# Diagonal score blocks of the recurrent pairs made in the projection phase, with the first four half pairs inverted there on GpSimd

## The reference, cut to what matters

```python
def step(s, inp):
    r_t, w_t, k_t, v_t, a_t, b_t = inp
    sa = jnp.einsum('bhvk,bhk->bhv', s, a_t)
    s = s * w_t[:, :, None, :] + sa[..., None] * b_t[:, :, None, :] + v_t[..., None] * k_t[:, :, None, :]
    return s, jnp.einsum('bhvk,bhk->bhv', s, r_t)
```

## Time and profile before

| | |
|---|---|
| median of 3 runs | 3104.68 us (3103.49 to 3105.19) |
| span of the profiled execution | 3097.4 us |
| median less that span | 7.3 us |
| PE busy | 2577.9 us, 83% |
| DVE busy | 1596.9 us, 52% |
| GpSimd busy | 740.9 us, 24% |
| granted clock of PE, mean | 0.902 |

### The profile page before, as it was taken

One profiled execution on the slowest core, in us unless ns is written; L12 is line 12 of the kernel. 1 busy time (PEld: TensorE's weight loads), 2 busy tenths in 40 slices (PEclk: granted clock), 3 DMA queues, 4 the chain that ended last, 5 costly groups with the idle time before them and its releaser, 6 DMA issues. The chain is left out here.

```text
span 3097.4 us, 54814 instructions
## 1 busy us (share of the span) xinstructions
PE 2577.9 (83%) x23550; PEld 2183.5 (70%) x23550; DVE 1596.9 (52%) x2411; ACT 902.7 (29%) x1464; POOL 740.9 (24%) x739
## 2 busy tenths in 40 slices
PE   6899999974788854676775999999599999998787
PEld 2577677764677753456564777877499999998665
DVE  3037887542435624785465556465544546454233
ACT  2114333311132222563202232222233333332211
POOL 1111111116556641111322111111021111111421
PEclk8999999986889887677887999999799999999898
DMA  6622555532324313121461323232402222210521
GB/s 263 223 65 80 165 146 158 165 129 77 80 73 127 103 30 97 37 54 32 155 133 55 112 97 116 97 109 99 176 35 76 89 76 90 76 55 2 220 94 60
DMA packets 291551, 319.51 MB, mean 103 GB/s; under 512 B 109807, under 2 KB 235190, under 8 KB 288750
## 3 DMA queue, kind: packets, MB, share of 16 engines
q1 hardware_dynamic: 290240, 312.64, 31.7%
q10 hardware_dynamic: 1070, 3.37, 0.3%
HBM read 203.32 MB, written 112.56 MB: 102 GB/s over the span
## 5 line engine op out<-in xcount | busy, mean ns | idle before, releaser
L2893 PE MATMUL PS<-Q,K 128*128 128x128 f32 x2560 | 296.3, 278 | 32.4 <-DMA K<-k_d 23.7
L2893 PEld LDWEIGHTS PS<-Q,K 128*128 128x128 f32 x2560 | 292.9, 194 | 34.9 <-issue 27.8
L3014 POOL TENSOR_TENSOR weights_lo<-weights,weights_hi 128x1664 fp32r<-128x1664 f32 x32 | 121.3, 3790 | 566.5 <-ACT weights_hi L2972 566.5
L2920 PE MATMUL PS<-V_hi,weights_hi 128*128 128x258 f32 x832 | 239.1, 287 | 5.4 <-DVE H L3123 2.7
L461 PE MATMUL PS<-hT_hi,w_in_hi 128*128 128x512 f32 (+1 forms) x640 | 239.7, 374 | 0.0
L462 PE MATMUL PS<-hT_lo,w_in_hi 128*128 128x512 f32 (+1 forms) x640 | 236.4, 369 | 0.0
L463 PE MATMUL PS<-hT_hi,w_in_lo 128*128 128x512 f32 (+1 forms) x640 | 236.2, 369 | 0.0
L2921 PE MATMUL PS<-V_lo,weights_hi 128*128 128x258 f32 x832 | 236.0, 284 | 0.0
L2922 PE MATMUL PS<-V_hi,weights_lo 128*128 128x258 f32 x832 | 235.3, 283 | 0.0
L461 PE MATMUL PS<-h_hi,w_in_hi 128*128 128x512 f32 (+1 forms) x624 | 228.5, 366 | 5.3 <-PEq L112 5.3
L2394 PE MATMUL PS<-w_out_hi,y_in_hi 128*128 128x512 f32 x416 | 169.0, 406 | 70.4 <-DVE y_in_lo L2332 39.1
(11 more groups left out here) (412 smaller groups left out, 5681.6 us busy)
## 6 DMA issues: line engine op xcount, KB each, us to landing
chunk_in<-in_d SPq DMA_DIRECT2D x40, 512.0 KB, 3.4
w_in<-in_e_w_in_dram SPq DMA_DIRECT2D x30, 512.0 KB, 5.0
xnew<-in_o_w_in_dram SPq DMA_DIRECT2D x30, 512.0 KB, 6.1
in_d<-xnat SPq DMA_DIRECT2D x20, 640.0 KB, 6.0
modw<-in_mod_w_dram SPq DMA_DIRECT2D x12, 1024.0 KB, 9.9
xnat<-in_mod_w_dram SPq DMA_DIRECT2D x8, 1536.0 KB, 7.2
v_d<-xnew SPq DMA_DIRECT2D x16, 640.0 KB, 3.0
k_d<-xc SPq DMA_DIRECT2D x16, 640.0 KB, 2.9
```

Source lines behind the costliest of these rows:

```text
L2893: last = pe.matmul(PS[:, 4 + x % 4, (j - j0) * P:(j - j0 + 1) * P], K[:, kt, j * P:(j + 1) * P], Q[:, kt, i * P:(i + 1) * P], start=(kt == ...
L2920: pe.matmul(out, wh, VH[:, j, q], start=(j == seen[0]), stop=False)
L3014: pool.tensor_tensor(WL[n % 2][:], W[:, n % 2], WH[n % 2][:].bitcast(F32), ALU.subtract).then_inc(s["w_lo"], 1)
```

## The change

The diagonal blocks are made a second time, in the projection phase: PE multiplies the 32-token blocks directly (`block_product`, `blk0` in tile b+4 and `blk1` in tile b+5), DVE masks them into `blocks_out` (`blocks`), and SP stores them (`blocks_away`). GpSimd inverts half pairs 0 to 3 there, ten of the 30 steps behind the low part of each tile from 13 to 24 (`invert`), with SP moving blocks in and results out (`inversion_io`). In the pair stage, `blocks_in` only loads (inverses for n below 4, blocks from 4 on), the transposed copy L1559 is gone, returning the blocks to `N` is a function of its own (`blocks_back`), and the inversion of half n+4 is started in turn n. The constants are cut into other pieces, so the masks of the pair stage are loaded at its start. The diff, cut:

```diff
-    PREP_PE[_b, 0], PREP_PE[_b, 1] = [("w0", _p)], [("a0", _p)]
+    PREP_PE[_b, 0], PREP_PE[_b, 1] = [("w0", _p)], [("a0", _p)] + ([("blk1", _p - 1)] if _p else [])
     PREP_PE[_b, 2] = [("bonus", _p - 1)] if _p else []
     PREP_PE[_b + 1, 0], PREP_PE[_b + 1, 1], PREP_PE[_b + 1, 2] = [("w1", _p)], [("a1", _p)], [("ksum", _p)]
+    PREP_PE[_b + 4, 1] = [("blk0", _p)]
+PREP_PE[PREP_AT + 4 * PREP_TILES, 1] = [("blk1", 3)]
...
-PREP_SEQ = [(name, p, i) for key in sorted(PREP_PE) for name, p in PREP_PE[key] for i in range(3)]
+PREP_SEQ = [(name, p, i) for key in sorted(PREP_PE) for name, p in PREP_PE[key] for i in range(2 if name[0:3] == "blk" else 3)]
...
+EARLY_HALVES = 4
+INVERT_AT, INVERT_TILES = 13, 3
+INVERT_STEPS = 30
...
+def invert_steps(pool, step, U, tmp, first, end, done=None, value=0):
+    for k in range(first, end, -1):
+        w = 31 - k
+        prod = tmp[0:104, 0:k * w].rearrange("b (i j) -> b i j", i=k)
+        step.link(pool.tensor_tensor(prod, U[0:104, 0:k, k:k + 1].broadcast_to([104, k, w]),
+                                     U[0:104, k:k + 1, k + 1:32].broadcast_to([104, k, w]), ALU.mult))
+        ins = pool.tensor_tensor(U[0:104, 0:k, k + 1:32], U[0:104, 0:k, k + 1:32], prod, ALU.add)
+        if k > 1:
+            step.link(ins)
+        else:
+            step.publish(ins, done, value)
...
+        U, blk = sb("early_blocks", [P, 32, 32]), sb("blocks_out", [P, NCH, 2, 32])
+        inv_tmp = G.c("pick")
...
+                def blocks_away(p, d):
+                    sp.wait_ge(s["by_dve"], BY_DVE.index((f"blk{d}", p, 1)) + 1)
+                    for i in range(2):
+                        for k in range(4):
+                            sp.dma_start(A.blk_d[2 * p + i, d, 10 * k:10 * k + 10].rearrange("b s t -> s b t"),
+                                         blk[32 * k:32 * k + 32, 5 * i:5 * i + 5].rearrange("s c h t -> s (c h) t")).then_inc(s["blk_st"], 16)
...
+                def inversion_io(n):
+                    i, at = divmod(n - INVERT_AT + 1, INVERT_TILES)
+                    if at or i < 0 or i > EARLY_HALVES:
+                        return
+                    if i:
+                        sp.wait_ge(s["inv_ok"], i)
+                        for d in range(2):
+                            sp.dma_start(A.inv_d[i - 1, d].rearrange("b s t -> b (s t)"),
+                                         U[64 * d:64 * d + 40].rearrange("b s t -> b (s t)")).then_inc(s["inv_st"], 16)
+                    if i < EARLY_HALVES:
+                        sp.wait_ge(s["blk_st"], 16 * 16 * (i // 2 + 1))
+                        if i:
+                            sp.wait_ge(s["inv_st"], 32 * i)
+                        else:
+                            sp.wait_ge(s["u_zero"], 1)
+                        for d in range(2):
+                            sp.dma_start(U[64 * d:64 * d + 40].rearrange("b s t -> b (s t)"),
+                                         A.blk_d[i, d].rearrange("b s t -> b (s t)")).then_inc(s["inv_in"], 16)
...
+                    if k < 2 and p:
+                        blocks_away(p - 1, k)
...
+                    inversion_io(n)
+                blocks_away(3, 1)
...
+                def block_product(p, d):
+                    ops = (aa[0], sg[0]) if d == 0 else (sg[1], kk)
+                    for h in range(2):
+                        x, bank = piece_of(f"blk{d}", p, h)
+                        bank_free(x)
+                        q = slice(64 * h, 64 * h + 64)
+                        for c in range(NCH):
+                            for k in range(4):
+                                t = slice(c * CH + 32 * k, c * CH + 32 * k + 32)
+                                ins = pe.matmul(PS[32 * k:32 * k + 32, bank, 32 * c:32 * c + 32], ops[0][q, t], ops[1][q, t],
+                                                start=True, stop=True)
+                        ins.then_inc(s["pp_ps"], 1)
...
+                            if name == "blk0":
+                                pe.wait_ge(ready[0], 4 * p + 3)
+                                block_product(p, 0)
+                            elif name == "blk1":
+                                pe.wait_ge(ready[1], 4 * p + 2)
+                                block_product(p, 1)
+                            else:
...
+                def invert(n):
+                    i, part = divmod(n - INVERT_AT, INVERT_TILES)
+                    if i < 0 or i >= EARLY_HALVES:
+                        return
+                    if part == 0:
+                        pool.wait_ge(s["inv_in"], 32 * (i + 1))
+                        inv_step.link(unit_diagonal(pool, U))
+                    each = INVERT_STEPS // INVERT_TILES
+                    invert_steps(pool, inv_step, U, inv_tmp, INVERT_STEPS - each * part, INVERT_STEPS - each * (part + 1), s["inv_ok"], i + 1)
...
+                pool.memset(U[:], 0.0).then_inc(s["u_zero"], 1)
                 for n in range(1, last + 1):
                     pool.wait_ge(s["hi_ok"], n)
                     pool.tensor_tensor(wl[n % 2][:], w[:, n % 2], wh[n % 2][:].bitcast(F32), ALU.subtract).then_inc(s["lo_ok"], 1)
+                    invert(n)
...
+                def blocks(p, d):
+                    if p or d:
+                        dve.wait_ge(s["blk_st"], 128 * (2 * p + d))
+                    for h in range(2):
+                        x, bank = piece_of(f"blk{d}", p, h)
+                        dve.wait_ge(s["pp_ps"], x + 1)
+                        dve.tensor_tensor(blk[:, :, h], PS[:, bank, 0:32 * NCH].rearrange("p (c t) -> p c t", t=32),
+                                          G.c("tri")[:, None, :].broadcast_to([P, NCH, 32]), ALU.mult).then_inc(s["by_dve"], 1)
...
+                        blocks(p - 1, 1)
...
+                        blocks(p, 0)
...
                 def blocks_in(n):
-                    sp.wait_ge(s["bx_sb"], HC * (n + 1))
+                    sp.wait_ge(s["zt_ok"], n)
+                    if n > EARLY_HALVES:
+                        sp.wait_ge(s["zu_st"], 32 * (n - EARLY_HALVES))
+                    src = A.inv_d if n < EARLY_HALVES else A.blk_d
                     for d in range(2):
-                        for k in range(4):
-                            sp.dma_start(A.blk_d[n, d, 10 * k:10 * k + 10].rearrange("b s t -> s b t"),
-                                         diag(d, n, k, k).rearrange("s c h t -> s (c h) t")).then_inc(s["rel_st"], 16)
-                    sp.wait_ge(s["rel_st"], 128 * (n + 1))
-                    if n:
-                        sp.wait_ge(s["zu_st"], 32 * n)
-                        sp.wait_ge(s["zt_st"], 32 * n)
-                    for d, dst in enumerate((U, Ut)):
-                        sp.dma_start(dst[64 * d:64 * d + 40].rearrange("b s t -> b (s t)"),
-                                     A.blk_d[n, d].rearrange("b s t -> b (s t)")).then_inc(s["rel_in"], 16)
+                        sp.dma_start(U[64 * d:64 * d + 40].rearrange("b s t -> b (s t)"),
+                                     src[n, d].rearrange("b s t -> b (s t)")).then_inc(s["rel_in"], 16)
...
-                    sp.wait_ge(s["inv_ok"], n + 1)
-                    away(U, A.inv_d, s["zu_st"])
+                    if n >= EARLY_HALVES:
+                        sp.wait_ge(s["inv_ok"], n - EARLY_HALVES + 1)
+                        away(U, A.inv_d, s["zu_st"])
                     sp.wait_ge(s["zt_ok"], n + 1)
                     away(Ut, A.invt_d, s["zt_st"])
...
+                    sp.wait_ge(s["bx_sb"], HC * (n + 1))
                     if n:
                         sp.wait_ge(s["y64_ps"], n)
-                    sp.wait_ge(s["zu_st"], 32 * (n + 1))
+                    else:
+                        sp.wait_ge(s["zero"], 4)
+                    if n >= EARLY_HALVES:
+                        sp.wait_ge(s["zu_st"], 32 * (n - EARLY_HALVES + 1))
...
+                sp.dma_start(G.cst_rwkv[:], A.consts[:, G.ends[3]:G.ends[4]]).then_inc(s["consts"], 16)
                 for m in half_chunks(0):
                     load(m)
+                sp.wait_ge(s["zero"], 1)
+                for d in range(2):
+                    sp.dma_start(U[64 * d:64 * d + 40].rearrange("b s t -> b (s t)"),
+                                 A.inv_d[0, d].rearrange("b s t -> b (s t)")).then_inc(s["rel_in"], 16)
...
-                sp.wait_ge(s["zero"], 4)
+                for n in range(EARLY_HALVES):
+                    blocks_out(n)
+                    blocks_in(n + 1)
+                blocks_back(0)
                 sp.wait_ge(s["wa_zero"], 1)
-                blocks_in(0)
-                blocks_out(0)
...
-                    if n + 1 < HALVES:
-                        blocks_in(n + 1)
...
-                        blocks_out(n + 1)
+                        blocks_back(n + 1)
+                    if n + EARLY_HALVES < HALVES:
+                        blocks_out(n + EARLY_HALVES)
+                        if n + EARLY_HALVES + 1 < HALVES:
```

(41 more changed lines are left out.)

52 lines of the change are left out of this document (31 added, 21 removed).

## The result

The changed kernel takes 3130.86 us (median of 4 runs, 3128.47 to 3132.05) against 3104.93 us before in the same measurement: the ratio is 1.0083 with a 95% interval of 1.0070 to 1.0096, so it is 26 us slower. The forecast was 13 us faster, and 3130.86 lies above the range's end of 3125, 39 us above the forecast of 3092.

The account below looks back on a forecast made before the run. PE bounds the projection nearly end to end, while the pair stage has 172 us of idle PE, 89.7 of it waiting for inverted blocks. 3097.4 - 113 (gain) + 100 (loss) + 7.3 gave 3092 us, range 3055 to 3125.

Parts of the forecast that it names:

- the 7.3 us around the span: Whole kernel: the median lies 7.3 us above the profiled span, so this was added to the predicted span of 3084.4.
- all seven waits gone: Pair stage: all seven PE waits of `y32` for the inverted blocks vanish, a gain of 89.7 us.
- The clock's gain of 16: Pair stage: PE's clock recovers where waits had lowered it, a gain of 16 us, bounds 0 and 28.
- the 4 us for DVE instructions beside GpSimd: Pair stage: ten DVE instructions that PE waits for run faster without GpSimd beside them, a gain of 4 us.
- The 4.3 us for DVE's first mask: Start of the pair stage: 3.5 of the 4.3 us that PE waits for DVE's first mask go.
- second step (GpSimd): Projection: inversion steps stretched beside DVE's preparation delay low parts at tiles 14, 15, 18 and 19, a loss of 22 + 18.
- low part late in nearly every tile: Projection, tiles 14 to 25: all eight other low parts late by 4 us, loss 132, time 3124; chance 0.20.
- First step (the gate weights): Projection, SP queue: gate weight loads behind block stores come 19.6, 17.7 and 11.0 us later, together 48.
- Third step (products): Projection, PE: 16 sets of 80 products of 32x32 cost 16 us, bounds 9 to 34.
- the rival without overlap: Projection, PE: the small products do not overlap in the array, 34 us instead of 16, time 3110; chance 0.08.
- Fourth step (DVE): Projection: GpSimd steps lengthen DVE's work by 57 to 67 us, of which 14 delay PE, bounds 0 to 57.
- Fifth step (clock): Projection: two new waits of over ten us lower PE's clock, 5 us lost in each: 10, bounds 0 and 20.

Follow-up runs that it names:

- f4_back_first: The changed kernel with the return of half pair 0's blocks moved behind the first of SP's four opening rounds instead of behind all four: 3112.42 us.
- e2_short_dve: The changed kernel with DVE's preparation steps k = 3 and 4, and its token mixing from tile 13 on, on 64 columns instead of 1280: 3068.12 us.
- e1_no_steps: The changed kernel without GpSimd's 240 inversion steps in the projection phase; loads, stores and semaphores stay: 3077.45 us.
- f2_one_gate: The changed kernel with one half pair inverted early over ten tiles, gate weight loads before block stores, and one half ahead in the pair stage: 3040.69 us.
- e3_gate_first: The changed kernel with SP issuing the four gate weight loads ahead of the eight block stores: 3115.36 us.

## Why the prediction was wrong, step by step

It was wrong on both sides of a difference of two large terms: the gain was 93 and not 113, the loss 124 and not 100. Either error alone, 20 or 24 us, is more than the 13 us that were forecast. A third, small one goes the other way, the 7.3 us around the span: the profiled execution of the change took 3132.05 us with a span of 3130.2, so a run is 1.85 us longer than its span, and the other 5.5 say that the profiled execution of before was that much shorter than the median. Together, 20 + 24 - 5.5 are the 39 us between forecast and result.

**The gain.** The mechanism was right: the waits for the inverse went from 89.7 to 12.2 us. The step that failed is "all seven waits gone". I checked the slack of `blocks_back(n+1)` in the middle of the stage, which held, and not that of `blocks_back(0)`, which SP issues behind four opening rounds; it came 43 us after the first product. f4_back_first shows it: 12.2 us and 5 of clock. The clock's gain of 16 was nearer 10: PE is busy 397.5 us instead of 407.0, at 0.90 instead of 0.84. Of the 4 us for DVE instructions beside GpSimd nothing shows: PE's waits for `S_rwkv` are 17.0 us where they were 16.8. The 4.3 us for DVE's first mask are gone (3.5 forecast).

**The loss, second step (GpSimd).** This is the term that failed. The stretching of the steps was foreseen and is shown by e2_short_dve, and 24.9 us for 20 steps is near the 30 I gave. What failed is the count of places. I put late low parts at tiles 14 and 15, and 18 and 19, and let them overlap with the gate waits, at 4 and 7 us above them. They came at seven tiles, 14, 15, 17, 18, 19, 23 and 24, 69.3 us and 2.9 more, because pair 3 is prepared beside half 3's inversion too (tiles 23 and 24, 17.2 us), and because GpSimd stands at the load of the next half's blocks with a low part queued behind it. I named what is queued behind SP's waits and not what is queued behind GpSimd's. Gate and low part waits together, with 2.5 us inside a tile, grew by 80 where I had 60. In the order of the forecast: up to pair 1's gates 10.9 us came for 20, at tiles 14 and 15 with pair 2's gates 24.1 for 22, at tiles 18 and 19 with pair 3's gates 17.4 for 18. Where I had counted, then, the sizes held or were smaller; tiles 17, 23 and 24, for which the forecast had nothing, brought 25.3. The rival "low part late in nearly every tile" was the nearest to what happened: its threshold of 113 was passed. But its condition was not met: seven tiles of twelve were late, and three new places brought 25 us, where it had 4 us at each of eight.

**First step (the gate weights).** The chain was right, its size too large. It had the first pair's weights at 356.8 us, and PE's product began at 354.60; but I compared that with the start of before, 337.17, as if PE came as early. PE came at 340.9, where it came at 334.4 before, since the block products and their waits had delayed it already (about 5 us at 325.9 to 331.1). So e1_no_steps, which has this step without late low parts, shows 41.1 us of gate waits where 12.0 had been, 29 more and not 48; with late low parts 17.6, 6 more. And the DMA was not the only path from that DVE instruction to PE: with the loads first, the PSUM bank waited for the same mask, up to 25.9 us (f2_one_gate).

**Third step (products).** 16 sets were predicted at 16 us. In the change 160 products, two sets, take 1.57 us:

```profile
370.63 1.57 PE L888 MATMUL PS<-pair_bufs,xnat 64*32 64x32 f32 x160 [0.25 <-ACT xnat L958]
```

That is 12.6 us for all, plus some 6 us of waits beside them (L888). The row at low clock with side by side tiles was the right one, and the rival without overlap falls. (The row has 40 products; the other 40 of the 80, of `inv_other`, lie between them in the same 1.3 us.)

**Fourth step (DVE).** 14 us were taken from 57 to 67 us of lengthening. DVE is busy 302.8 us in the projection of the change and 294.5 in e1_no_steps: the steps lengthen it by 8 us in all. What of it reached PE is some 2 us, its waits for DVE's `pair_bufs` (7.4 us where they were 5.8). The 0.38 us of the earlier trace rows was not what a step costs DVE on the mean; the price of sharing fell on GpSimd, 60 us. The Trainium skill's rule, page "SBUF — State Buffer", section "🔬 SBUF: two separate sides", that one of the two fully blocks the other, agrees with the low parts (DVE's instruction 3.69 us beside one, its neighbour 1.48) and with GpSimd's steps, which take DVE's 1.8 us; the estimate of 88 us for DVE that I drew from it is eleven times what was measured. It was also worked out with 0.5 us a step, where the mean step in the prediction is 0.6 (35.8 us for 60), which would have given 106; and the lower value of 0.32 us in the fourth step stands in none of the rows.

**Fifth step (clock).** 10 us were predicted; PE's busy time grew by 30, of which 12.6 are products, so 17 are put down to the clock. I had counted two new waits of over ten us; there are five, and one of 8. The 5 us for each fit what the trace shows behind the 13.7 us wait at 354.60: a granted clock of 0.50, 0.50 and 0.68 in the three windows of 4 us up to 366, and 1.00 in the next. Six of these would be 30 us and not 17; some stand where the kernel before had a stall already, and the rest is not shown. Last, the opening of the pair stage took 6 us more (13.6 to 19.6 us of waiting for chunks), which I had not counted.

So the loss was 80 (waits for gate weights and low parts) + 19 (products and the waits beside them) + 2 (DVE) + 17 (clock) + 6 (opening) = 124, where the forecast had 60 + 16 + 14 + 10.

## What to carry to other kernels

Work moved to an engine that "has time" is paid in latency there: ask what is queued behind each of its waits and steps, in every tile where it stands, and who needs that next. Move as little as hides the wait: here one half pair early, six instructions a tile instead of 20, did as well as two, the runs with none early were slower by 10 us at most, and the rest ran in the stage that had the slack. When one event holds the critical engine by two paths (here a DMA and a PSUM bank), taking one away shows only the other; move the event itself.

## What the runs showed of the hardware

A GpSimd step of 104 partitions takes 0.53 us on the mean beside short DVE instructions (e2_short_dve) and 0.79 in a phase with 1280-column ones (e3_gate_first), up to 1.8 us where DVE runs without a pause, in step with it one to one (433 to 439 us of the change); DVE's own 1.49 us become 1.8 in that stretch. Summed over the phase, GpSimd lost 60 us and DVE 8. 160 products of 32x32 with 64 rows of contraction took 1.57 us at a granted clock of 1.00. I had expected the greater part on DVE.
